# The down projection of a decoder layer: two passes over the output columns, 13 of 44 pairs of k tiles by Strassen's seven block products, low parts on VectorE

## The reference

```
h = RMSNorm(x); p = h @ W_in                     # q, k, v, gates
y = concat[DiffAttn(p_da), GLA(p_gla)] @ W_out;  x = x + RMSNorm(y)
h = RMSNorm(x); [a, u] = causal dwconv3(h @ W_up)
y = (silu(a) * u) @ W_down;                      x = x + RMSNorm(y)
return x[:, 16:]
```

## Time and profile before

| | us |
|---|---|
| median of 3 runs | 1214.57 |
| the profiled execution, its own time | 1214.44 |
| its span in the trace | 1212.3 |
| TensorE busy | 1198.7 (99% of the span) |
| VectorE busy | 662.1 (55%) |
| ScalarE busy | 612.3 (51%) |
| GpSimd busy | 483.0 (40%) |

### The profile page before, as it was taken

One profiled execution on the slowest core, in us unless ns is written; L12 is line 12 of the kernel. 1 busy time (PEld: TensorE's weight loads), 2 busy tenths in 40 slices (PEclk: granted clock), 3 DMA queues, 4 the chain that ended last, 5 costly groups with the idle time before them and its releaser, 6 DMA issues.

```text
span 1212.3 us, 23685 instructions
## 1 busy us (share of the span) xinstructions
PE 1198.7 (99%) x8918; PEld 1141.7 (94%) x8918; DVE 662.1 (55%) x959; ACT 612.3 (51%) x918; POOL 483.0 (40%) x227
## 2 busy tenths in 40 slices
PE   9999999999999999999999999999999999999997
PEld 9999999999999999999999999999999988888885
DVE  7765555454564456766666666666656733232234
ACT  7544445455684447644454445444544544444444
POOL 1233333333434433444444444444444444444443
PEclk9999999999999999999999999999999999999999
DMA  9655554544446555556656565565655565565641
GB/s 339 193 158 156 142 161 141 150 141 141 138 134 204 181 161 173 176 168 191 181 181 184 179 184 176 177 190 173 190 183 166 193 202 188 193 194 188 200 163 70
DMA packets 172751, 212.31 MB, mean 175 GB/s; under 512 B 6688, under 2 KB 158624, under 8 KB 172576
## 3 DMA queue, kind: packets, MB, share of 16 engines
q1 hardware_dynamic: 172272, 210.32, 56.3%
q10 hardware_dynamic: 432, 1.34, 0.3%
HBM read 209.53 MB, written 2.10 MB: 175 GB/s over the span
## 4 chain that ended last, share of the span: by engine, by line
PE 95%; ACT 2%; DVE 1%; issue 1%; DMA 1%; SPq 0%; DVEq 0%; ACTq 0%
PE psum L441 70%; PE psum L1823 19%; PE psum L1462 1%; PE psum L1693 1%; DMA raw<-in_w_first 1%; PE psum L1522 1%; PE psum L1851 0%; PE psum L1548 0%; PE psum L1783 0%; PE psum L1626 0%; PE psum L1644 0%; ACT w_hi L421 0%; PE psum L1549 0%; PE psum L1639 0%; DVE proj L1438 0%
## 5 line engine op out<-in xcount | busy, mean ns | idle before, releaser
L425 POOL TENSOR_TENSOR w_lo<-raw,w_hi 128x1024 fp32r<-128x1024 f32 x188 | 464.8, 2472 | 702.5 <-ACT w_hi L421 702.5
L441 PE MATMUL psum<-a_hi,w_hi 128*128 128x258 f32 (+1 forms) x2360 | 675.1, 286 | 0.9 <-ACT temp L629 0.8
L441 PE MATMUL psum<-a_lo,w_hi 128*128 128x258 f32 (+1 forms) x2360 | 674.2, 286 | 0.0
L441 PE MATMUL psum<-a_hi,w_lo 128*128 128x258 f32 (+1 forms) x2360 | 671.4, 284 | 0.0
L421 ACT ACTIVATE w_hi<-raw 128x1024 fp32r<-128x1024 f32 x391 | 411.5, 1058 | 455.9 <-PE psum L441 327.2
L425 DVE TENSOR_TENSOR w_lo<-raw,w_hi 128x1024 fp32r<-128x1024 f32 x204 | 268.0, 1315 | 402.8 <-ACT w_hi L421 401.7
L441 PEld LDWEIGHTS psum<-a_hi,w_hi 128*128 128x128 f32 x2360 | 449.1, 190 | 6.6 <-issue 3.9
L441 PEld LDWEIGHTS psum<-a_lo,w_hi 128*128 128x128 f32 x2360 | 449.4, 190 | 0.0
L441 PEld LDWEIGHTS psum<-a_hi,w_lo 128*128 128x128 f32 x2360 | 447.0, 189 | 0.1
L1352 DVE SCALAR_TENSOR_TENSOR proj<-proj,par 128x256 f32<-128x256 f32 x88 | 111.6, 1268 | 38.2 <-ACT proj L848 38.2
L1823 PE MATMUL psum<-w_hi,a_hi 128*128 128x512 f32 x336 | 130.9, 390 | 0.0
(11 more groups left out here) (240 smaller groups left out, 613.9 us busy)
## 6 DMA issues: line engine op xcount, KB each, us to landing
raw<-in_w_up SPq DMA_DIRECT2D x176, 512.0 KB, 3.6
raw<-in_w_in SPq DMA_DIRECT2D x88, 512.0 KB, 4.2
raw<-in_w_down SPq DMA_DIRECT2D x88, 512.0 KB, 4.1
raw<-in_w_out SPq DMA_DIRECT2D x32, 512.0 KB, 3.6
raw<-in_w_first SPq DMA_DIRECT2D x7, 512.0 KB, 11.1
xT<-in_features SPq DMA_DIRECT2D x3, 544.0 KB, 7.8
temp<-in_post_ffn_g ACTq DMA_DIRECT2D x1, 1024.0 KB, 4.7
out<-proj SPq DMA_DIRECT2D x2, 512.0 KB, 2.7
```

Source lines behind the costliest of these rows:

```text
L425: eng.tensor_tensor(w_lo[:, j % SPLIT, :], raw[:, j, :], w_hi[:, j % SPLIT, :], ALU.subtract)\
L441: mm = pe.matmul(psum[:, bank + m, 0:t1 - t0], w[:, j % SPLIT, cols], a[:, k, t0:t1], start=(k == 0 and step == 0), stop=(k == KT - 1 and ...
```

## The change

The output columns are made in two passes of 1024 columns (`half` 0 and 1). In each pass the 44 k tiles are taken as 22 pairs; `PASSES` lists them, `s` a plain pair and `S` a pair by Strassen's seven products: 6 in the first pass, 7 in the second. A plain pair is two chunks of 12 products each, as before. A pair with two token tiles, two k tiles and two column halves is a 2 x 2 by 2 x 2 block product, which takes seven block products of 3 matrix products each, 21 in place of 24. For it

- VectorE makes four sums and differences of activation blocks, once for 7 pairs, in an iteration in the middle of the up projection (`pair_sum`); ScalarE and VectorE split the seven forms (896 columns, `form_hi`, `form_lo`) into slots of their own, 9 times in all; four pairs keep theirs from the first pass to the second.
- VectorE makes four differences of 128 x 512 weight blocks (`differences`) while it treats the pair that stands ahead. A pair S so has four units of weights of 1024, 1024, 1024 and 512 columns, used by 6, 6, 6 and 3 products. A unit takes a slot of `w_hi` and `w_lo`, as a chunk does.
- all low parts of weights are made on VectorE; GpSimd makes none in this stage from chunk 4 on.
- four of the block products are added up in banks of their own. Two pairs after the last S of a pass, ScalarE copies one and VectorE makes four additions (`prepare`) to what the outputs still lack.

A pass uses 4 banks for its outputs and the other 4 for those products. The second pass wants the output banks of the first for its products: before its first S, VectorE adds the two parts of the first pass's output and ScalarE squares them (with its writes into those banks), and TensorE waits for the second of these squares. The loops of this stage are now written out. At the end (`final_banks`) the last two plain pairs go together.

```diff
+PASSES = ("ss" + "Sss" * 5 + "Sssss", "ss" + "SsSss" * 3 + "Sssss")
+SEVEN = ((0, 1, 2, 3, 4, 5), (2, 3, 4, 5, 0, 1, 6))
...
+def down_pairs(n_pairs):
+    pairs, unit, plain, seventh = [], 0, 0, 0
+    for half, kinds in enumerate(PASSES):
+        sevens, others = list(SEVEN[half]), [n for n in range(n_pairs) if n not in SEVEN[half]]
+        for place, kind in enumerate(kinds):
+            n = (sevens if kind == "S" else others).pop(0)
+            form, at = FORM_AT[half][n] if kind == "S" else (0, 0)
+            pairs.append(Pair(half, kind == "S", n, unit, 2 * len(pairs), plain, seventh, form, at, place))
+            unit += 4 if kind == "S" else 2
+            plain += 0 if kind == "S" else 2
+            seventh += 1 if kind == "S" else 0
+    return pairs
...
+        pair_act = proj[:, 0:N_SUMS * 4 * P].rearrange("p (n b t) -> p n b t", n=N_SUMS, b=4)
+        pair_sums = xT[:].rearrange("p k t -> p (k t)")[:, 0:N_SUMS * 4 * P].rearrange("p (n b t) -> p n b t", n=N_SUMS, b=4)
+        w_diff = proj[:, CV0:CV0 + 3 * BANK]
+        rests = (F_FIRST, F_SECOND)
...
+        def unit_source(pr, n):
+            return raw_of(pr.chunk + n) if n < 2 else w_diff[:, 0:CHUNK] if n == 2 else w_diff[:, CHUNK:]
+        def unit_hi(eng, pr, n):
+            u = pr.unit + n
+            src = unit_source(pr, n)
+            eng.wait_ge(chunk_used, UP1 + u - SPLIT + 1)
+            if n < 2:
+                await_landed(eng, pr.chunk + n)
+            if pr.seven and n > 0:
+                eng.wait_ge(diffs_ready, 2 * pr.seventh + min(n, 2))
+            eng.activation(w_unit(w_hi, u)[:, 0:src.shape[1]], src, ACT.Copy).then_inc(hi_ready, 1)
+        def unit_lo(eng, pr, n):
+            u = pr.unit + n
+            src = unit_source(pr, n)
+            eng.wait_ge(hi_ready, UP1 + u + 1)
+            eng.tensor_tensor(w_unit(w_lo, u)[:, 0:src.shape[1]], src, w_unit(w_hi, u)[:, 0:src.shape[1]], ALU.subtract)\
+               .then_inc(d_w_ready, 1)
...
+            for c in range(2 * len(DOWN)):
+                kt, half = chunk_rows(c)
...
+                    u = unit_of(c - RAW)
...
+                        sp.wait_ge(d_w_ready, u - SPLIT + 1)
...
+                sp.dma_start(raw_of(c), w_down[0, kt * P:(kt + 1) * P, half * CHUNK:(half + 1) * CHUNK])\
+                    .then_inc(raw_landed[c % RAW], 16)
...
+            def form_hi(pr):
+                act_e.wait_ge(sums_made, 4)
+                for src, f in ((pair_act[:, pr.pair, 1:4, :], slice(0, 3)), (pair_sums[:, pr.pair], slice(3, 7))):
+                    ins = copy(f_hi[:, pr.at, f, :], src)
+                ins.then_inc(form_hi_ready, 1)
...
+            for pr in DOWN:
+                if pr.place == LAST_SEVEN + 2:
+                    act_e.wait_ge(chunk_used, UP1 + pr.unit - 2)
+                    copy(rests[pr.half][1][:, 0:BANK], product(pr.half, 0)).then_inc(one_copied, 1)
+                for n in range(4 if pr.seven else 2):
+                    if pr.unit + n >= SPLIT:
+                        unit_hi(act_e, pr, n)
+                    if not pr.seven and pr is not DOWN[0]:
+                        down_hi(pr, n)
+                    if pr.seven and n == 0 and (pr.half == 0 or pr.form > max(f for f, _ in FORM_AT[0].values())):
+                        form_hi(pr)
+                if pr.half == 1 and pr.place == 2:
+                    for t in range(2):
+                        act_e.wait_ge(f_added, t + 1)
+                        f_square(banks(out_bank(0, t, 0), out_bank(0, t, 0) + 2), F_FIRST[t], 3 * t)
...
+            def form_lo(pr):
+                dve.wait_ge(form_hi_ready, pr.form + 1)
+                for src, f in ((pair_act[:, pr.pair, 1:4, :], slice(0, 3)), (pair_sums[:, pr.pair], slice(3, 7))):
+                    ins = dve.tensor_tensor(f_lo[:, pr.at, f, :], src, f_hi[:, pr.at, f, :], ALU.subtract)
+                ins.then_inc(form_ready, 1)
+            def differences(pr, part):
+                b2, b1 = raw_of(pr.chunk), raw_of(pr.chunk + 1)
+                if part == 0:
+                    for c in (pr.chunk, pr.chunk + 1):
+                        await_landed(dve, c)
...
+                    dve.tensor_tensor(w_diff[:, 0:BANK], b1[:, BANK:], b1[:, 0:BANK], ALU.subtract).then_inc(diff_step, 1)
+                    dve.wait_ge(diff_step, 2 * pr.seventh + 1)
+                    dve.tensor_tensor(b1[:, BANK:], b2[:, BANK:], b1[:, BANK:], ALU.subtract).then_inc(diffs_ready, 1)
+                else:
+                    dve.wait_ge(diff_step, 2 * pr.seventh + 1)
+                    dve.tensor_tensor(w_diff[:, BANK:CHUNK], b2[:, BANK:], w_diff[:, 0:BANK], ALU.subtract)\
+                        .then_inc(diff_step, 1)
+                    dve.wait_ge(diff_step, 2 * pr.seventh + 2)
+                    dve.tensor_tensor(w_diff[:, CHUNK:], b2[:, 0:BANK], w_diff[:, BANK:CHUNK], ALU.subtract)\
+                        .then_inc(diffs_ready, 1)
+            def prepare(pr):
+                five, six, seven = (product(pr.half, n) for n in (1, 2, 3))
+                (three, whole), (one, four) = ((r[:, 0:BANK], r[:, BANK:]) for r in rests[pr.half])
+                dve.wait_ge(one_copied, pr.half + 1)
+                dve.wait_ge(chunk_used, UP1 + pr.unit)
+                for n, (dst, a, b) in enumerate(((four, six, one), (three, seven, four), (four, five, four),
+                                                 (whole, five, three))):
+                    if n > 0:
+                        dve.wait_ge(prep_step, 4 * pr.half + n)
+                    dve.tensor_tensor(dst, a, b, ALU.add).then_inc(prep_step, 1)
...
+            for p, pr in enumerate(DOWN):
+                following = DOWN[p + 1] if p + 1 < len(DOWN) else None
+                if pr.place == LAST_SEVEN + 2:
+                    prepare(DOWN[p - 1])
+                if pr.half == 1 and pr.place == 2:
+                    for t in range(2):
...
+                        src = banks(out_bank(0, t, 0), out_bank(0, t, 0) + 2)
+                        dve.tensor_tensor(F_FIRST[t], src, F_FIRST[t], ALU.add).then_inc(f_added, 1)
+                for n in range(4 if pr.seven else 2):
+                    if pr.unit + n >= SPLIT:
+                        unit_lo(dve, pr, n)
+                    if following and following.seven and not pr.seven:
+                        differences(following, n)
+                    if not pr.seven and pr is not DOWN[0]:
+                        down_lo(pr, n)
+                    if pr.seven and n == 0 and (pr.half == 0 or pr.form > max(f for f, _ in FORM_AT[0].values())):
+                        form_lo(pr)
...
+            def f_add(t, col):
+                dve.wait_ge(banks_done, 3 + 2 * t + col + 1)
+                piece = f_piece(t, col)
+                dve.tensor_tensor(piece, f_bank(t, col), piece, ALU.add).then_inc(f_added, 1)
             dve.wait_ge(g_row_landed, 16)
+            dve.wait_ge(prep_step, 8)
+            for t in range(2):
+                f_gain(banks(F_BANK[t], F_BANK[t] + 2), F_FIRST[t], 0, 2)
+            f_add(0, 0)
+            f_gain(f_bank(0, 0), f_piece(0, 0), CHUNK, 3)
+            f_add(0, 1)
+            f_mean_square(f_ms[:, 0:1], 0, 3, 4)
+            f_gain(f_bank(0, 1), f_piece(0, 1), CHUNK + BANK, 4)
             f_reciprocal(0)
+            f_final(F_FIRST[0], banks(F_BANK[0], F_BANK[0] + 2), x1_nat[:, 0, 0:CHUNK], 0, 1)
+            gained = [banks(F_BANK[0] + n, F_BANK[0] + n + 1) for n in range(2)]
+            for n in range(2):
+                dve.wait_ge(f_done, 1)
+                f_add(1, n)
+                dve.wait_ge(f_added, 2 + 2 + n + 1)
+                f_gain(gained[n], f_piece(1, n), CHUNK + n * BANK, 4)
+                if n == 0:
+                    f_mean_square(f_part[:], 3, 5, 5)
             f_reciprocal(1)
+            f_final(F_FIRST[1][:, BANK:], banks(F_BANK[1] + 1, F_BANK[1] + 2), x1_nat[:, 1, BANK:CHUNK], 1, 2)
+            for n in range(2):
+                if n == 1:
+                    dve.wait_ge(f_ss_ready, 6)
+                f_final(f_piece(1, n), gained[n],
+                        x1_nat[:, 1, CHUNK + n * BANK:CHUNK + (n + 1) * BANK], 1, 5 + n)
...
+            def seven_products(pr):
+                first, last = pr.place == PASSES[pr.half].index("S"), pr.place == LAST_SEVEN
+                one, five, six, seven = (product_bank(pr.half, n) for n in range(4))
+                out = lambda t, n: out_bank(pr.half, t, n)
+                pe.wait_ge(form_ready, pr.form + 1)
+                for n, products in enumerate((
+                        ((2, out(1, 0), 0), (6, out(1, 1), 1)), ((0, one, 0), (5, seven, 1)),
+                        ((3, five, 0), (4, six, 1)), ((1, out(0, 0), 0),))):
+                    await_unit(pr.unit + n)
+                    for form, bank, col in products:
+                        own = first and bank // 4 == pr.half
+                        for k, (a, w) in enumerate(((f_hi, w_hi), (f_lo, w_hi), (f_hi, w_lo))):
```

(103 more changed lines are left out.)

231 lines of the change are left out of this document (102 added, 129 removed).

## The result

The changed kernel takes 1224.03 us (median of 4 runs, 1223.19 to 1224.80) against 1214.32 of the kernel before: ratio 1.0081, 95% interval 1.0069 to 1.0093. It is slower by 9.7 us. The forecast was 1219.9 with a range up to 1223.2: the direction was right, the size too small by 4.1 us, and the time lies outside the range. Only the fastest of the four runs has a trace, and what follows is read from it.

The account below looks back on a forecast made before the run. TensorE's row of products was taken to bound the kernel: -8.84 us for fewer products, +12.0 for pauses and restarts, +2.3 for the tail, sum +5.5 on 1214.44, giving 1219.9 us; range 1214.6 to 1223.2.

Parts of the forecast that it names:

- The products: Down projection on TensorE: 39 fewer products at an unchanged distance of 0.2267 us save 8.84 us.
- Rival 1: TensorE's products go faster without GpSimd and with loops written out, giving back 13.6 us: 1206.3; chance 0.07.
- The four activation sums: VectorE in an up projection iteration: about 1.0 us each, fitting into its free time, costing nothing.
- The four pauses: TensorE waits at stage start 2.7, lone pairs 3.0, banks' change of hands 3.0, last two pairs 2.7 us more.
- the lone pairs: Three plain pairs between two S in the second pass: TensorE waits for activation low parts, three times 1.0 us.
- rival 2: TensorE's clock falls to half after three pauses near 3 us, 2.5 us each, 7.5 together: 1227.4; chance 0.08.
- The tail: Norm and stores behind the last product: 10.3 us in place of 8.0, +2.3; bounds 0 and +3.5.
- T: The end of TensorE's last product, from which the tail's times are counted; final pieces were forecast at T+4.0.

Follow-up runs that it names:

- e3: The changed kernel with ScalarE making the two squares of the first pass's output before the third high part, not behind the fourth: 1220.74 us.
- e1: The changed kernel with the activation's low part ahead of the next S's weight differences on VectorE: 1219.02 us.
- e2: The changed kernel with the wait before the last 48 products split, the last pair's activation low parts awaited only after 12 products: 1220.42 us.
- t1: The changed kernel with two tail edits, root's table loaded before the last squares and second token tile's first piece added before the first's final piece: 1221.14 us.
- p1: The kernel before with one more TensorE wait, for activation low parts, in each of nine down projection iterations, pauses of 2.90 us: 1249.92 us.
- e4: The changed kernel with the three edits of e1, e2 and e3 together: 1210.98 us.
- e5: The changed kernel with the edits of e4 and t1 together: 1208.88 us.
- p2: The kernel before with one more TensorE wait, for chunk 4's high part on ScalarE, in each of nine iterations, pauses of 1.31 us: 1227.41 us.

## Why the forecast was wrong

**The products: right.** 39 fewer at 0.2267 us, and the distance does not change without GpSimd or with the loops written out (48 products in 10.88 us, over and over). Rival 1 is out. VectorE had room on average, as summed: 69.3 us busy in 80. The four activation sums cost nothing, as forecast: the stage starts at 963.94, where it was 964.12.

**The four pauses: right, within 0.1 us for three.** 2.68 for the forecast 2.7, 2.96 for 3.0, 2.90 for 2.98. For the lone pairs I wrote 3 x 1.0; the trace has 0.13, 0.93 and 0.93, the first hidden by the half clock ahead of it (e3 brings it back). e1, e2 and e3 show the causes: each edit removes the pause that its wait made (of the first, 1.35 stays), and what comes up in their place is 0.40 in e1 and the lone pair's 0.93 in e3.

**The step that failed: rival 2, the clock's fall, left out of the sum with a chance of 0.08.** It was the normal case. In the changed kernel's profiled execution it came behind two of three long pauses; counted over the profiled executions of all kernels here, behind 15 of 21 pauses of 2.7 to 3.0 us (2 of 3 here, 2 of 2 each in e1, e2 and e3, 1 of 3 in t1, 6 of 9 in p1) and behind none of the nine of 1.3 nor the three of 1.35 in e1, e4 and e5. I had drawn from the earlier trace rows that 5 us idle precede a fall. That is what happened once at the end; here a pause of 2.7 us was enough. A single long delay told me nothing of the shortest one. It is not even a constant: in the eleven profiled executions here the clock falls 2.0 to 5.2 us after the last product has ended. The earliest is e1's, where it ended at 1206.51:

```profile
1206.50:1218.60 12.10, 0.01 (x1) 0.00 (x0) 5.74 (x11) 3.43 (x7) 4.06 (x2) 0.58 0.46 173
```

0.58 over these 12.1 us is 10.2 us at half, so it fell near 1208.4, 2 us idle. The kernel before shows one of the longest of these delays. The price was too high on the other side: 2.5 us from the start's products, while a stretch lasts 3.41 us and costs 1.6. Two of them make 3.2 us, beside the missing 4.1; the runs of 1224.7 and 1224.8, beside 1223.2 and 1223.4, would fit a third one behind the last pause, but only the run of 1223.19 has a trace, so that stays open.

**The tail: the term was mis-sized.** I wrote +2.3 with 3.5 as its upper bound; it is +4.1 (12.1 against 8.0). The walk itself was close: the final pieces start at T+4.3 (forecast T+4.0), GpSimd ends at T+7.1 (T+7.6). With the 3.1 us behind the last piece, T+7.6 would have made 10.7, not the 10.3 that I took. What was wrong was that 3.1, taken over from a kernel whose stores were spread out. With five stores in a burst it is 5.0: the last one is issued 1.2 us behind the last piece, and lands 0.8 later after its issue than before. In t1 2.4 of the growth of 4.1 go, with GpSimd's first piece 2.2 us earlier and the burst dissolved; the two are not told apart.

Together: -0.9 (lone pairs) + 3.2 (clock) + 1.8 (tail) = +4.1 on the forecast of +5.5, 9.6 in all. The spans of the two profiled executions differ by 9.2, their own times by 8.75 (the changed kernel has 1.7 us around its span and not 2.1), the medians by 9.7. The sum so fits the spans to 0.4; that the medians are 1 us further apart than the profiled times is the spread of the changed kernel's runs. Without the clock's 3.2 the time would have been 1220.8, within the range. The forecast's direction rested on a sum of 12.0 against 8.84; with the pauses taken out (e4) the removal does show: the last product starts 7.3 us earlier than in the kernel before.

The Trainium skill's rule that I cited beside rival 2 ("TensorE: Matmul & The Clock Gate", section "HAM oscillation — how this bites in real kernels") says that idle gaps between bursts put the array back to half rate. p1 bears it out, six times of nine at 2.90 us, and p2 shows no fall at 1.31; it was the better guide than my reading of the earlier trace rows. What the Trainium skill gives beside rival 1 (the same page, section "Wait — 56ns, not 53.3ns?"), 215.7 ns from start to start, is not borne out here: the undisturbed distance is 226.7 ns before and after the change.

## What to carry over

A wait that stops the bounding engine should be priced twice, for its length and for what the clock does behind it: here nine pauses of 1.3 us cost 13 us, nine of 2.9 cost 35.5. When work is moved onto an engine that has room on average, walk its program order at each hand-over: here the three edits of e4, each for a small result or a wait that stood in the wrong place, gave back 13.1 us, where 39 products fewer save 8.84; and reordering, with one small instruction more for the root's table and none less, turned +9.7 us into -6.5. And stores that become ready late leave in a burst: each stands behind the one before it and lands later, so the last piece's distance to the end is not a constant of the kernel.

## What the hardware showed that I had not expected

- The granted clock goes to half behind pauses of 2.7 to 3.0 us of TensorE, 15 times of 21, for stretches of 3.41 us, and the stretch costs 1.3 to 1.7 us of products of 512 columns (1.3 in e3, 1.7 in p1). It never did behind pauses of 1.3 us (9 of 9 held) or 1.35 (3 of 3). After the last product it held for 2.0 to 5.2 us, with nothing in the tail's timing to go with it: 2.0 in e1 and 5.0 in the changed kernel, whose tails are alike.
- In p1 the falls follow a pattern (two, none, two, none, one, none, one), with pauses of one length. That the same kernel has several times, 1248.2 to 1251.4, would fit another number of falls in each; only the run of 1251.36 has a trace.
- A slower TensorE hides a late VectorE: the first lone pair's pause was 0.13 to 0.23 us behind a half-clock stretch (three traces) and 0.93 without one (e3).
